# Two changes to one kernel: the last quarter of x is turned by VectorE and moved by transfers, and the first transfers wait for one another

## The chip, the cores and the metric

The kernel runs on one core of one Trainium2 chip. A core has TensorE (PE), VectorE (DVE), ScalarE (ACT), GpSimd (POOL) and SyncE (SP), each with its own instruction queue, and 16 DMA engines that all queues share. The time is device microseconds of one execution. The kernel before takes 2688.36 us, the median of 3 runs (2688.32 to 2688.46).

## The reference, cut to what matters

Everything is float32, with 256 tokens of 2048 features. Two layers (a mixer and an MLP each) are followed by one hybrid layer of attention and gating. What matters here is that each of the five stages begins by normalizing x and multiplying it by a large weight matrix:

```python
def rms_norm(x, g):
    xf = x.astype(jnp.float32)
    y = xf * lax.rsqrt(jnp.mean(xf * xf, axis=-1, keepdims=True) + EPS)
    return (y * g.astype(jnp.float32)).astype(x.dtype)

def sq_relu_mlp(h, w1, w2):
    a = jax.nn.relu(jnp.einsum("btd,df->btf", h, w1))
    return jnp.einsum("btf,fd->btd", a * a, w2)

def first_block(x, ...):
    for layer in range(DEPTH):                       # DEPTH = 2
        h = rms_norm(x, mix_pre_g[layer])
        if layer % 2 == 0:
            m = pool_conformer_mixer(h, ...)         # window means, a causal convolution of 31 taps, layer norm, silu
        else:
            m = short_conv_mixer(h, ...)             # gates and a causal convolution of 3 taps
        x = x + rms_norm(m, mix_post_g[layer])
        h = rms_norm(x, ffn_pre_g[layer])
        x = x + rms_norm(sq_relu_mlp(h, ffn_w1[layer], ffn_w2[layer]), ffn_post_g[layer])
    return x

def hybrid_layer(x, norm_g, w_in, ...):
    proj = rms_norm_2(x, norm_g) @ w_in              # 2048 x 11264
    ...                                              # attention of 8 heads, spatial gating
    return x + merged @ w_out
```

## The kernel before

**Stages, chunks and steps.** The work on TensorE is 160 chunks of 512 output columns, in five stages: stage 0 is the first mixer, 1 its MLP, 2 the second mixer, 3 its MLP, 4 the hybrid layer. A chunk contracts 1024 or 2048 rows of a weight matrix in steps of 256 rows (`STEP_K = 2` blocks of 128). `SEQ` is the list of all steps (chunk, i), `POS` the place of a step in it, and a stage's first step is called f here. In stages 1 to 4 the first two chunks are interleaved: f to f+3 are steps 0 to 3 of the first, f+4 to f+7 steps 0 to 3 of the second, f+8 to f+11 steps 4 to 7 of the first, f+12 to f+15 those of the second.

**The exact product.** Each float32 operand is held as a rounded part (hi) and the rest (lo), and a product is three matmuls (L786 to L788): `w_hi` by `A_lo`, `w_lo` by `A_hi`, `w_hi` by `A_hi`. For each of the 2 token tiles and 2 blocks that makes 12 matmuls of 512 columns in a step. ScalarE makes `w_hi` (`split_hi`, L747), VectorE `w_lo` (`split_lo`, L765), in 6 slots; both run 3 steps ahead of the step that they stand at (`split_steps`, `AHEAD`). Some steps are split in two halves (L735, L755), those in `HALVED` among them. SyncE loads two steps at a time (1 MB) into 3 slots (`load_weights`, L627), each load behind a wait on `lo_made` for the slot's last use. `load_rows` (L637) loads 128 rows (256 KB) with a semaphore of its own.

**The left operand.** x lies token by token in SBUF; `A_hi` and `A_lo` need it feature by feature and scaled by the gain. Its 2048 features are 4 groups of 512 (g = 0 to 3). TensorE transposes a group in 16 blocks of 128x128 for stages 1 to 4, groups 0 and 1 tile by tile in `boundary` (L854), groups 2 and 3 by `turn_x` (8 each, L837) between steps: group 2 behind step f+4, group 3 behind step f+6. ScalarE reads the bank and writes `A_hi` (`hi_x`, L1083 and L1084), VectorE writes `A_lo` (`lo_x`, L1468). Group 2 is first used in step f+8, group 3 in step f+10. At step f+8 ScalarE also runs `statistics` (L1125), the sums of squares of the two tiles.

**What sets the order.** It is written out by hand: every engine's program walks the same list of steps and does its extra work at named (chunk, i). Engines meet on semaphores alone. In hidden layers VectorE also transposes 32x32 blocks itself (`turn_blocks`, L1839): one instruction takes 32 partitions and puts the result on another 32, 16 of them for a group.

**The opening.** SyncE issues the first transfers one behind the other with no wait: the rows of steps 0 to 3 by `load_rows`, quarters of x by `load_x` (L614), one load of 1 MB in two pieces, then 14 small transfers of parameters (L659 to L673), and only then the load of steps 6 and 7, which waits for `lo_made` too. ScalarE's queue issues one transfer, the first eighth of x (L1162). TensorE transposes the parameters (13 transfers) behind step 5 of chunk 0.

**The convolution's end.** In chunks 6 to 9 of stage 0 VectorE's last taps (`DVE_TAP_TO` = 58), the layer norm at (8, 2) and the silu at (9, 1) and (10, 0) have their places; TensorE transposes the convolution's result for the norm behind (8, 2), at L940.

Of the kernel before, what the change touches and what calls it, by code (L numbers as in the profile page):

```python
# [251 lines left out]
def build(nc, t):  # L252
    ctx = ExitStack()
    with ctx:
# [62 lines left out]
        for name in ("A", "B"):  # L317
            halves[name] = tuple(sbuf(f"{name}_{h}", D // P * TOK, F32R).rearrange("p (k t) -> p k t", t=TOK)
                                 for h in ("hi", "lo"))
# [52 lines left out]
        x_begun = semaphore("x_begun")  # L372


        BEGIN = 2 * STEPS_PER_LOAD
        rows_loaded = [semaphore(f"rows_loaded{i}") for i in range(2 * GK)]
# [235 lines left out]
        def sync_program(e):  # L612
# [47 lines left out]
            e.dma_start(rows[32:64, 0:P], t["ffn_pre_g"].rearrange("l (k p) -> (l k) p", p=P)).then_inc(par_loaded, 16)  # L660
            for name, key in (("norm_g_2", "pre2"), ("pool_scale", "pool_scale"), ("conv_b", "conv_b"),
                              ("conv_ln_g", "ln_g"), ("conv_ln_b", "ln_b"), ("q_norm_g_2", "q_g"), ("k_norm_g_2", "k_g")):
                n = t[name].shape[1] // P
# [1511 lines left out]
```

## Time and profile before

| what | value |
|---|---|
| median of 3 runs | 2688.36 us (2688.32 to 2688.46) |
| the profiled execution's own time | 2690.7 us |
| its span, first to last instruction | 2689.0 us |
| granted TensorE clock | 1.000 of full speed |
| TensorE busy | 2679.8 us, 12001 matmuls (weight loads 2218.5 us beside them) |
| VectorE busy | 1872.4 us (70%) |
| ScalarE busy | 1292.8 us (48%) |
| GpSimd busy | 278.2 us (10%) |
| DMA | 515.58 MB, mean 192 GB/s; SyncE's queue fills 55.4% of the 16 engines' span |

TensorE is busy in every one of the page's 40 slices at 90% or more. The difference between the profiled execution and the median is 2.3 us, and the span leaves 1.7 us of the execution outside. A matmul's end is modelled, so a row's duration overlaps the next row's start; the pace is read from start to start.

### The profile page before, as it was taken

What the parts mean: (1) busy time and instruction counts of PE and PEld (TensorE: products, weight loads), DVE (VectorE), ACT (ScalarE), POOL (GpSimd) and SP (SyncE); (2) the same over time, 40 slices, a digit from 0 to 9 for tenths busy, and PEclk for the clock granted to TensorE, in tenths of its full rate; (3) what the DMA queues carried; (4) which work ended last, traced back from release to release, by engine and by line L of the source; (5) the groups of instructions that cost most, each with busy time, mean ns of one, the idle gap of its engine ahead of it and who ended that gap; (6) DMA issues with size and microseconds to landing.
All of it is one profiled execution on the core that took longest, in us unless ns stands there. A gap on an engine that the chain in (4) does not pass through costs nothing.

```text
span 2689.0 us, 31099 instructions
## 1 busy us (share of the span) xinstructions
PE 2679.8 (100%) x12001; PEld 2218.5 (83%) x12001; DVE 1872.4 (70%) x2495; ACT 1292.8 (48%) x1635; POOL 278.2 (10%) x263
## 2 busy tenths in 40 slices
PE   9999999999999999999999999999999999999999
PEld 7888888888888888888888888888888888888887
DVE  6878777666866767776677676667767757765564
ACT  6765544434444454444544444344445446544452
POOL 4851100000000010000110000000011001000000
PEclk9999999999999999999999999999999999999999
DMA  7545665555555556555555555555555645455554
GB/s 248 183 169 180 215 211 183 184 202 188 193 192 195 194 183 213 193 197 194 187 188 204 203 188 186 190 188 203 188 188 179 211 173 182 169 200 194 188 188 156
DMA packets 267972, 515.58 MB, mean 192 GB/s; under 512 B 8450, under 2 KB 27956, under 8 KB 267316
## 3 DMA queue, kind: packets, MB, share of 16 engines
q1 hardware_dynamic: 267556, 513.34, 55.4%
q8 instruction: 98, 1.61, 0.2%
q14 instruction: 46, 0.38, 0.0%
q10 hardware_dynamic: 272, 0.26, 0.0%
HBM read 511.47 MB, written 2.10 MB: 191 GB/s over the span
## 4 chain that ended last, share of the span: by engine, by line
PE 98%; DMA 1%; DVE 1%; ACT 0%; issue 0%; SPq 0%
PE bank L786 32%; PE bank L788 32%; PE bank L787 32%; PE bank L837 1%; DMA x_res<-in_x 0%; DMA w_raw<-in_ab_w_in 0%; PE bank L854 0%; PE bank L1027 0%; DVE w_lo L765 0%; PE bank L988 0%; PE bank L1041 0%; PE bank L1014 0%; DVE w_lo L755 0%; DVE bank L1783 0%; PE bank L1048 0%
## 5 line engine op out<-in xcount | busy, mean ns | idle before, releaser
L765 DVE TENSOR_TENSOR w_lo<-w_raw,w_hi 128x1024 fp32r<-128x1024 f32 x952 | 1183.1, 1265 | 493.5 <-ACT w_hi L747 487.8
L747 ACT ACTIVATE w_hi<-w_raw 128x1024 fp32r<-128x1024 f32 x956 | 974.7, 1056 | 589.9 <-PE bank L788 432.9
L786 PE MATMUL bank<-w_hi,A_lo 128*128 128x512 f32 x2432 | 952.5, 392 | 2.3 <-DVE A_lo L1468 0.8
L788 PE MATMUL bank<-w_hi,A_hi 128*128 128x512 f32 x2432 | 947.2, 389 | 0.0
L787 PE MATMUL bank<-w_lo,A_hi 128*128 128x512 f32 x2432 | 946.7, 389 | 0.0
L786 PE MATMUL bank<-w_hi,B_lo 128*128 128x512 f32 x1408 | 548.7, 390 | 0.0
L788 PE MATMUL bank<-w_hi,B_hi 128*128 128x512 f32 x1408 | 547.9, 389 | 0.0
L787 PE MATMUL bank<-w_lo,B_hi 128*128 128x512 f32 x1408 | 547.8, 389 | 0.0
L786 PEld LDWEIGHTS bank<-w_hi,A_lo 128*128 128x128 f32 x2432 | 456.6, 188 | 98.4 <-DVE w_lo L765 2.3
L788 PEld LDWEIGHTS bank<-w_hi,A_hi 128*128 128x128 f32 x2432 | 456.4, 188 | 95.8
L787 PEld LDWEIGHTS bank<-w_lo,A_hi 128*128 128x128 f32 x2432 | 456.7, 188 | 93.2
L788 PEld LDWEIGHTS bank<-w_hi,B_hi 128*128 128x128 f32 x1408 | 264.3, 188 | 54.9
L786 PEld LDWEIGHTS bank<-w_hi,B_lo 128*128 128x128 f32 x1408 | 264.3, 188 | 54.7
L787 PEld LDWEIGHTS bank<-w_lo,B_hi 128*128 128x128 f32 x1408 | 264.3, 188 | 54.6
L1072 ACT ACTIVATE z<-bank,small 128x512 f32<-128x512 f32 x108 | 68.4, 685 | 341.9 <-PE bank L788 341.8
L1839 DVE STREAM_TRANSPOSE conv_out<-z 32x256 f32<-32x256 f32 x512 | 222.9, 435 | 10.5
L2131 POOL TENSOR_TENSOR z<-z 128x512 f32<-128x512 f32 x64 | 65.2, 1040 | 1105.5 <-ACT z L1072 1105.5
L1866 DVE TENSOR_TENSOR acc<-bank,acc 128x512 f32<-128x512 f32 x96 | 61.9, 686 | 85.7 <-PE bank L788 85.7
L2012 POOL TENSOR_TENSOR acc<-acc,gain_row 128x512 f32<-128x512 f32 x32 | 40.9, 1294 | 518.7 <-ACT bank L1131 483.5
L1425 ACT ACTIVATE B_hi<-conv_out 128x512 fp32r<-128x512 f32 x64 | 37.0, 628 | 100.2 <-DVE conv_out L1839 100.2
L1131 ACT ACTIVATE bank<-acc 128x512 f32<-128x512 f32 x32 | 19.0, 595 | 79.9 <-DVE acc L1521 51.1
L2006 POOL TENSOR_TENSOR small<-small,neg_half 128x1 f32<-128x1 f32 (+2 forms) x21 | 23.3, 1110 | 307.8 <-DVE small L1460 288.9
(178 smaller groups left out, 975.7 us busy)
## 6 DMA issues: line engine op xcount, KB each, us to landing
w_raw<-in_ffn_w SPq DMA_DIRECT2D x256, 1024.0 KB, 5.1
w_raw<-in_w_in SPq DMA_DIRECT2D x88, 1024.0 KB, 4.9
w_raw<-in_sc_w_in SPq DMA_DIRECT2D x48, 1024.0 KB, 5.1
w_raw<-in_ab_w_out SPq DMA_DIRECT2D x16, 1024.0 KB, 5.0
w_raw<-in_sc_w_out SPq DMA_DIRECT2D x16, 1024.0 KB, 5.1
w_raw<-in_w_out SPq DMA_DIRECT2D x16, 1024.0 KB, 5.3
w_raw<-in_ab_w_in SPq DMA_DIRECT2D x28, 512.0 KB, 4.6
w_raw<-in_ab_w_in SPq DMA_DIRECT2D x8, 1024.0 KB, 5.1
```

The source lines that it names most:

```text
L747: e.activation(w_hi[:, s % SPLIT_SLOTS, :], raw_step(s), ACT.Copy).then_inc(hi_made, 1)
L765: e.tensor_tensor(w_lo[:, slot, :], raw_step(s), w_hi[:, slot, :].bitcast(F32), ALU.subtract).then_inc(lo_made, 1)
L786: e.matmul(ps, lo[:, kt, tok], wh, start=first, stop=False)
L787: e.matmul(ps, hi[:, kt, tok], wl, start=False, stop=False)
L788: ins = e.matmul(ps, hi[:, kt, tok], wh, start=False, stop=last)
L837: ins = e.transpose(view[:, k, tt * P:(tt + 1) * P], src(tt, slice(f, f + P)), ident)
L1072: e.activation(out(tt), main_bank(c, tt), func, scale=rs(layer_of(c))[:, tt:tt + 1]).then_inc(act_took(c, tt), 1)
L1425: e.activation(halves["B"][0][:, kt:kt + 2, :], h_T[:, 2 * h:2 * h + 2, :], ACT.Copy).then_inc(hi_cast("h", layer, b, j, h), 1)
L1839: ins = e.transpose(dst[feat, :, :].rearrange("p k (t c) -> p t k c", t=NT)[:, :, :, tok], src[tok, :, :].rearrange("p t (k c) -> p t k c" ...
L1866: e.tensor_tensor(out, main_bank(c, tt), out, ALU.add).then_inc(dve_took(c, tt), 1)
L2012: e.tensor_tensor(out, out, gain_row[:, c], ALU.mult).then_inc(gained(p, n, tt), 1)
L2131: e.tensor_tensor(z[:, s, tt, :], z[:, s, tt, :], z[:, s, tt, :], ALU.mult).then_inc(squared(layer, b, j, tt), 1)
```

## The change

**For stages 1 to 4, group 3 of x.** At the end of VectorE's `boundary` the new `turn_last` transposes it with 4 instructions on 128 partitions, each 32x32 block within its own band of 32 partitions, into `x_quads` (a part of `conv_in`). The new `move_x` then sends the 16 blocks of 32 partitions by 256 elements (32 KB each) to the bands where they belong, into `x_T` (a part of `conv_out`), from ScalarE's queue: 6 behind step f+4, 6 behind f+5, 4 behind f+6 in ScalarE's program. At step f+8 ScalarE waits for all 16 and makes `A_hi` (`hi_moved`, 4 activations from SBUF), VectorE makes `A_lo` (`lo_moved`, 8 instructions of 128x128), both ahead of the statistics. `turn_x(p, 3)` and the `hi_x`, `lo_x` of group 3 are gone, and two banks less are filled in a stage.

**In the opening**, most of SyncE's first transfers wait for an earlier one to have landed, the third load is made of `load_rows` too (so steps 4 and 5 are split in halves), and the parameters come behind the loads of steps 6 to 9. ScalarE and VectorE take the splits of steps 2 and 3 between the two halves of group 1. The parameters' transposes stand one step later.

**In stage 0's end**, VectorE does the last two steps' taps together one step earlier, its norm one step earlier, and the first silu is one step earlier on three engines.

```diff
     for key in turn_order():
+        if key[0] == "pre" and key[1] > 0 and key[2:3] == (NG - 1,):
+            continue
...
+        x_quads = conv_in_flat[:, 0:GK * TOK]
+        x_T = conv_out_flat[:, GK * TOK:2 * GK * TOK]
...
-        BEGIN = 2 * STEPS_PER_LOAD
+        BEGIN = RAW_SLOTS * STEPS_PER_LOAD
...
             load_rows(0, 0)
             load_rows(0, 1)
             e.dma_start(x[:, :, CH // 2:CH], x_dram[:, :, CH // 2:CH]).then_inc(x_loaded[0], 16)
+            e.wait_ge(x_begun, 16)
             load_rows(0, 2)
+            e.wait_ge(rows_loaded[0], 16)
             load_rows(0, 3)
+            e.wait_ge(rows_loaded[1], 16)
             load_x(1)
-            for k in range(GK):
-                load_rows(1, k)
+            e.wait_ge(x_loaded[0], 16)
+            load_rows(1, 0)
+            e.wait_ge(rows_loaded[2], 16)
+            load_rows(1, 1)
+            e.wait_ge(rows_loaded[3], 16)
+            load_rows(1, 2)
+            load_rows(1, 3)
+            e.wait_ge(x_loaded[1], 16)
             load_x(2)
-            load_weights(2)
+            e.wait_ge(rows_loaded[4], 16)
+            load_rows(2, 0)
...
+            e.wait_ge(x_loaded[2], 16)
             load_x(3)
-            e.dma_start(rows[0:32, 0:P], t["mix_pre_g"]...
...
             for n in range(RAW_SLOTS, LOADS):
                 load_weights(n)
+                if n == RAW_SLOTS + 1:
+                    load_params()
...
-                if (c, i) == (0, 5):
+                if (c, i) == (0, 6):
                     e.wait_ge(par_loaded, 16 * 13)
...
-                if c == up_chunk(layer, 0, 1) and i in (0, 2):
-                    turn_x(p, 2 + i // 2)
+                if (c, i) == (up_chunk(layer, 0, 1), 0):
+                    turn_x(p, 2)
...
+            def move_x(p, blocks):
+                e.wait_ge(x_turned.sem, x_turned.of(p))
+                for q, r in (divmod(m, 4) for m in blocks):
+                    e.dma_start(x_T[32 * r:32 * r + 32, q * TOK:(q + 1) * TOK],
+                                x_quads[32 * q:32 * q + 32, r * TOK:(r + 1) * TOK]).then_inc(x_moved, 16)
+            def hi_moved(p):
+                e.wait_ge(x_moved, 256 * p)
+                for k in range(GK):
+                    kt = GK * (NG - 1) + k
+                    ins = e.activation(by_32(halves["A"][0][:, kt, :]), moved(k), ACT.Copy, scale=par_col(PRE_COL[p], kt))
...
-                if (c, i) == (STAGE[p] + 1, 2):
-                    hi_x(p, 3)
+                if (c, i) in MOVE_AT[p]:
+                    move_x(p, MOVE_AT[p][c, i])
                 if (c, i) == (STAGE[p], 4):
+                    hi_moved(p)
                     statistics(p)
...
+        MOVE_AT = {p: {(STAGE[p] + 1, i): range(6 * i, min(6 * i + 6, 16)) for i in range(3)} for p in range(1, 5)}
...
+            def turn_last(p):
+                e.wait_ge(x_made.sem, x_made.of(p - 1, NG - 1, 1))
+                blocks = x[:, :, (NG - 1) * CH:].rearrange("p t (k c) -> p t k c", k=GK)
+                for r in range(4):
+                    out = x_quads[:, r * TOK:(r + 1) * TOK].rearrange("p (t k c) -> p t k c", t=NT, k=GK)
+                    ins = e.transpose(out, blocks[:, :, :, 32 * r:32 * r + 32])
+                ins.then_inc(x_turned(p), 1)
...
-                if (c, i) == (8, 2):
+                if (c, i) == (8, 1):
                     dve_norm(e, mean)
-                if (c, i) in ((9, 1), (10, 0)):
+                if (c, i) in ((9, 0), (10, 0)):
                     dve_silu(e, c - 9)
```

How the order of instructions moves is shown at three places. The first is ScalarE at the start of stage 1, from the end of group 2's `A_hi` to the statistics, before:

```order
210 L1084 ACTIVATE A_hi<-bank,par 128x256
211 L747 ACTIVATE w_hi<-w_raw 128x1024 x2
212 L1083 ACTIVATE A_hi<-bank,par 128x256
213 L1084 ACTIVATE A_hi<-bank,par 128x256
214 L1083 ACTIVATE A_hi<-bank,par 128x256
215 L1084 ACTIVATE A_hi<-bank,par 128x256
216 L747 ACTIVATE w_hi<-w_raw 128x1024 x2
217 L1125 ACTIVATE acc,small<-x_res 128x2048 x2
218 L747 ACTIVATE w_hi<-w_raw 128x1024 x3
```

And the same place in the changed kernel, where `conv_out` is `x_T` and `conv_in` is `x_quads`:

```order
211 L1111 ACTIVATE A_hi<-bank,par 128x256
212 L1125 DMA conv_out<-conv_in 32x256 x6
213 L774 ACTIVATE w_hi<-w_raw 128x1024
214 L1125 DMA conv_out<-conv_in 32x256 x6
215 L774 ACTIVATE w_hi<-w_raw 128x1024
216 L1125 DMA conv_out<-conv_in 32x256 x4
217 L774 ACTIVATE w_hi<-w_raw 128x1024 x2
218 L1133 ACTIVATE A_hi<-conv_out,par 128x256 x4
219 L1171 ACTIVATE acc,small<-x_res 128x2048 x2
220 L774 ACTIVATE w_hi<-w_raw 128x1024 x3
```

The 16 issues stand between the splits of weights, and the four activations of group 3 have moved behind four splits, directly ahead of the statistics. The second place is VectorE at the end of stage 1's boundary, before:

```order
175 L1543 SCALAR_TENSOR_TENSOR x_res<-acc,small,x_res 128x512 x2
176 L765 TENSOR_TENSOR w_lo<-w_raw,w_hi 128x1024
177 L1543 SCALAR_TENSOR_TENSOR x_res<-acc,small,x_res 128x512 x2
178 L765 TENSOR_TENSOR w_lo<-w_raw,w_hi 128x1024 x2
179 L1468 SCALAR_TENSOR_TENSOR A_lo<-bank,par,A_hi 128x256 x4
180 L765 TENSOR_TENSOR w_lo<-w_raw,w_hi 128x1024 x2
181 L1468 SCALAR_TENSOR_TENSOR A_lo<-bank,par,A_hi 128x256 x4
182 L765 TENSOR_TENSOR w_lo<-w_raw,w_hi 128x1024 x2
183 L1460 TENSOR_SCALAR small<-small 128x2
```

And the same place in the changed kernel:

```order
178 L1627 SCALAR_TENSOR_TENSOR x_res<-acc,small,x_res 128x512 x2
179 L1545 STREAM_TRANSPOSE conv_in<-x_res 128x256 x4
180 L792 TENSOR_TENSOR w_lo<-w_raw,w_hi 128x1024 x2
181 L1527 SCALAR_TENSOR_TENSOR A_lo<-bank,par,A_hi 128x256 x4
182 L792 TENSOR_TENSOR w_lo<-w_raw,w_hi 128x1024 x4
183 L1555 SCALAR_TENSOR_TENSOR A_lo<-conv_out,par,A_hi 128x128 x8
184 L1519 TENSOR_SCALAR small<-small 128x2
```

Four transposes stand ahead of the splits of steps f+6 and f+7, and group 3's `A_lo` is 8 smaller instructions behind step f+11's split. The third place is SyncE's opening, before:

```order
5 L614 DMA x_res<-in_x 128x2x512
6 L637 DMA w_raw<-in_ab_w_in 128x2x256 x4
7 L614 DMA x_res<-in_x 128x2x512
8 L627 DMA w_raw<-in_ab_w_in 128x4x256 x2
9 L614 DMA x_res<-in_x 128x2x512
10 L659 DMA z<-in_mix_pre_g 32x128
```

And in the changed kernel, with the semaphore that each issue waits for:

```order
4 L643 DMA w_raw<-in_ab_w_in 128x2x256 [waits x_begun]
5 L643 DMA w_raw<-in_ab_w_in 128x2x256 [waits rows_loaded0]
6 L620 DMA x_res<-in_x 128x2x512 [waits rows_loaded1]
7 L643 DMA w_raw<-in_ab_w_in 128x2x256 [waits x_loaded0]
8 L643 DMA w_raw<-in_ab_w_in 128x2x256 [waits rows_loaded2]
9 L643 DMA w_raw<-in_ab_w_in 128x2x256 [waits rows_loaded3]
10 L643 DMA w_raw<-in_ab_w_in 128x2x256
11 L620 DMA x_res<-in_x 128x2x512 [waits x_loaded1]
```

The order of the transfers of weights and x is the same; what is new are the waits, which leave some four transfers under way at a time.

## Rows read from the trace of the kernel before

**Rows 1.** The page's part 4: the chain that ended last.

```profile
PE 98%; DMA 1%; DVE 1%; ACT 0%; issue 0%; SPq 0%
```

**Rows 2.** TensorE's opening in the timeline: start us, us, instruction [idle before it].

```profile
7.12 0.50 PE L786 MATMUL bank<-w_hi,A_lo 128*128 128x512 f32 x1 [0.66 <-DVE w_lo L755]
...
10.50 0.40 PE L788 MATMUL bank<-w_hi,A_hi 128*128 128x512 f32 x1
12.63 1.09 PE L837 MATMUL bank<-ident,x_res 128*128 128x128 f32 x8 [1.73 <-DMA x_res<-in_x]
...
23.93 0.50 PE L786 MATMUL bank<-w_hi,A_lo 128*128 128x512 f32 x1 [0.67 <-DVE w_lo L765]
...
31.93 0.47 PE L786 MATMUL bank<-w_hi,A_lo 128*128 128x512 f32 x1 [0.81 <-DVE A_lo L1468]
...
34.77 0.39 PE L786 MATMUL bank<-w_hi,A_lo 128*128 128x512 f32 x1
```

**Rows 3.** DMA busy share in one stretch of the opening (windows view).

```profile
core 0: us, PE busy (x) PEld busy (x) DVE busy (x) ACT busy (x) POOL busy (x), PEclk, DMA share, GB/s
10.00:12.50 2.50, 0.90 (x4) 0.38 (x3) 1.72 (x4) 1.51 (x3) 2.21 (x12) 1.00 1.07 371
```

**Rows 4.** Transfers by line: size of one, median us from issue to landing.

```profile
w_raw<-in_ffn_w SPq DMA_DIRECT2D x256, 1024.0 KB, 5.1
...
out_x<-x_res SPq DMA_DIRECT2D x8, 256.0 KB, 2.1
x_res<-in_x SPq DMA_DIRECT2D x3, 512.0 KB, 8.8
...
x_res<-in_x ACTq DMA_DIRECT2D x1, 256.0 KB, 3.6
...
sgu_row<-in_sgu_norm_g SPq DMA_DIRECT2D x1, 64.0 KB, 6.2
```

**Rows 5.** SyncE's issues in the opening (timeline).

```profile
13.41 0.56 SPq L659 DMA_DIRECT2D z<-in_mix_pre_g  x1
14.02 0.42 SPq L660 DMA_DIRECT2D z<-in_ffn_pre_g  x1
14.48 0.43 SPq L664 DMA_DIRECT2D z<-in_norm_g  x1
...
18.84 37.86 SPq L627 DMA_DIRECT2D w_raw<-in_ab_w_in  x18
```

**Rows 6.** TensorE at the start of stage 1 (timeline).

```profile
267.60 1.03 PE L837 MATMUL bank<-ident,x_res 128*128 128x128 f32 x8
268.39 0.47 PE L786 MATMUL bank<-w_hi,A_lo 128*128 128x512 f32 x1
...
283.01 0.39 PE L786 MATMUL bank<-w_hi,A_lo 128*128 128x512 f32 x1
...
288.45 0.39 PE L786 MATMUL bank<-w_hi,A_lo 128*128 128x512 f32 x1
```

**Rows 7.** ScalarE: its one transfer, then the start of stage 1 (timeline).

```profile
0.80 0.44 ACTq L1162 DMA_DIRECT2D x_res<-in_x  x1
...
269.68 2.02 ACT L747 ACTIVATE w_hi<-w_raw 128x1024 fp32r<-128x1024 f32 x2
...
277.94 1.93 ACT L1125 ACTIVATE acc<-x_res 128x2048 f32<-128x2048 f32 x1
```

**Rows 8.** VectorE at the start of stage 1 (timeline).

```profile
267.24 2.36 DVE L765 TENSOR_TENSOR w_lo<-w_raw,w_hi 128x1024 fp32r<-128x1024 f32 x2
...
282.82 3.50 DVE L765 TENSOR_TENSOR w_lo<-w_raw,w_hi 128x1024 fp32r<-128x1024 f32 x3 [0.78 <-ACT w_hi L747]
```

**Rows 9.** Costliest groups, by line: count, busy us, mean ns of one.

```profile
L1839 DVE STREAM_TRANSPOSE conv_out<-z 32x256 f32<-32x256 f32 x512 | 222.9, 435 | 10.5
```

**Rows 10.** One line's instructions: ns min/median/max, first and last start.

```profile
L1483 DVE SCALAR_TENSOR_TENSOR A_lo<-bank,par,A_hi x64: 340/344/351, 251.3 to 2016.2; 128x128 fp32r<-128x128 f32 x64
```

**Rows 11.** Waits of TensorE: us in total, times, longest.

```profile
PE bank L940 <- DVE conv_out L1769: 0.3, 1, 0.3
```

More of the change, by code:

```diff
@@ L371, in build @@
         x_loaded = [semaphore(f"x_loaded{i}") for i in range(NG)]
[L372 to L376 removed]
+        x_begun, x_moved = semaphore("x_begun"), semaphore("x_moved")
+        BEGIN = RAW_SLOTS * STEPS_PER_LOAD
+        rows_loaded = [semaphore(f"rows_loaded{i}") for i in range(RAW_SLOTS * GK)]
         half_hi = semaphore("half_hi")
@@ L448, in build @@
                                    ([(g, tt) for tt in tiles for g in gs] if 0 in gs else [(g, tt) for g in gs for tt in tiles])])
+        x_turned = signal("x_turned", [(p,) for p in range(1, 5)])
         tap_done = signal("tap_done", DVE_TAPS)
@@ L660, in sync_program @@
[L660 to L663, printed above, removed]
-                e.dma_start(rows[ROWS[key]:ROWS[key] + n, 0:P],
-                            t[name].rearrange("l (k p) -> (l k) p", p=P)).then_inc(par_loaded, 16)
@@ L666, in sync_program @@
-            e.dma_start(rows[ROWS["b_spatial"]:ROWS["b_spatial"] + 8, 0:P], t["b_spatial_2"][0, :, :]).then_inc(par_loaded, 16)
-            taps = t["conv_w"].rearrange("l k (b p) -> (l k b) p", p=P)
-            for h in two:
-                e.dma_start(rows[0:CONV_ROWS, (1 + h) * P:(2 + h) * P],
-                            taps[h * CONV_ROWS:(h + 1) * CONV_ROWS, :]).then_inc(par_loaded, 16)
-            e.dma_start(rows[0:SHORT_ROWS, 3 * P:4 * P],
-                        t["sc_conv_w"].rearrange("l k (b p) -> (l k b) p", p=P)).then_inc(par_loaded, 16)
@@ L966, in pe_program @@
                 r = c - C_L2
-                if r == 1 and i in (0, 2):
-                    turn_x(4, 2 + i // 2)
+                if (r, i) == (1, 0):
+                    turn_x(4, 2)
                 if since(c, i, C_L2) == 3:
@@ L1170, in act_program @@
                 at[0] += 1
-            hi_x(0, 1)
+            for h in two:
+                hi_half(0, 1, h)
+                split_to(e, split_hi, at, STEPS_PER_LOAD + h)
             for c, i in split_steps(e, 0, split_hi, at):
@@ L1186, in act_program @@
                     hi_x(0, 2 + i // 4)
-                if (c, i) == (0, 5):
+                if (c, i) == (0, 6):
+                    statistics(0)
                     e.wait_ge(aux_filled.sem, aux_filled.of("rows"))
@@ L1470, in lo_scaled, with lo_half, lo_moved @@
                 ins.then_inc(lo_cast(*key), 1)
+            def lo_half(p, g, h):
+                kt = GK * g + 2 * h
+                lo_scaled("A", kt, [par_col(PRE_COL[p], kt + k) for k in two], "pre", p, g, h)
             def lo_x(p, g):
                 for h in two:
-                    kt = GK * g + 2 * h
-                    lo_scaled("A", kt, [par_col(PRE_COL[p], kt + k) for k in two], "pre", p, g, h)
+                    lo_half(p, g, h)
+            def turn_last(p):
[5 more added lines that the diff above has]
+                ins.then_inc(x_turned(p), 1)
+            def lo_moved(p):
+                hi, lo = halves["A"]
+                for k in range(GK):
+                    kt = GK * (NG - 1) + k
+                    e.wait_ge(hi_cast.sem, hi_cast.of("pre", p, NG - 1, k // 2))
+                    for tt in tiles:
+                        ins = e.scalar_tensor_tensor(by_32(lo[:, kt, :])[:, tt, :, :], moved(k)[:, tt, :, :],
+                                                     par_col(PRE_COL[p], kt), by_32(hi[:, kt, :].bitcast(F32))[:, tt, :, :],
+                                                     ALU.mult, ALU.subtract)
+                    if k % 2 == 1:
+                        ins.then_inc(lo_cast("pre", p, NG - 1, k // 2), 1)
             def lo_part(p, g, tt, h):
@@ L1589, in dve_program @@
                 at[0] += 1
-            lo_x(0, 1)
+            for h in two:
+                lo_half(0, 1, h)
+                split_to(e, split_lo, at, STEPS_PER_LOAD + h)
             for c, i in split_steps(e, 0, split_lo, at):
```

64 lines of the change are left out of this document (46 added, 18 removed).

## The prediction

> **What bounds the kernel now.** I read the chain that ended last first: 98% of the span is TensorE [rows 1]. So a change is worth only what it takes out of TensorE's stream, or what it stops TensorE from waiting for. The second view is TensorE's timeline, read from start to start. In stage 1, 24 matmuls lie between the starts 283.01 and 288.45 us [rows 6], 0.227 us each, so a step of 12 takes 2.72 us; there the stream has no holes. The third is the same view of the opening [rows 2]: between the first product at 7.12 and the start of the eighth step at 34.77 there are three waits, 1.73 us for x (group 1), 0.67 for `w_lo` and 0.81 for `A_lo`. The brackets count from a modelled end: the start at 10.50 and one pace of 0.23 give 10.73, and the next start is 12.63, so the hole is 1.90, 0.17 more than its bracket. With 0.17 added to each, the three are 1.9 + 0.84 + 0.98 = 3.7 us. One wait of 0.3 us stands at the end of stage 0, ahead of the norm's transposes [rows 11]. The fourth view is what the other engines do at a stage's start [rows 7, 8], since the change loads both.
>
> **The opening.** Before, the transfers are issued without waits and share the engines: the DMA share is 1.07 at 371 GB/s [rows 3], and a quarter of x (512 KB) takes 8.8 us to land, against 5.1 for 1 MB later [rows 4]. Group 1 lands late since later transfers move beside it. With the waits it is issued when the second 256 KB of weights has landed. From ScalarE's row, 256 KB land 3.6 us after issue [rows 4]; for the second row load, issued at about 1.8, I estimate 5.5, so group 1 goes out at about 5.9. Ahead of it and beside it are at most 1.25 MB issued from 4.4 on (0.80 + 3.6, the first landing). At 371 GB/s these take 3.4 us, and the fixed part of a landing is 2.1 less 0.7 of moving [rows 4], 1.4: it lands at 4.9 + 3.4 + 1.4 = 9.7. TensorE asks for it at about 10.5. So the first hole goes.
> The third hole goes too. The load of steps 6 and 7 is issued at 18.84 [rows 5], behind parameters whose issue began at 13.41; SyncE spent 5.4 us on 14 of them. Now it is issued when group 3 has been, by my estimate near 16, and TensorE needs it near 28. What is late next is step 4: VectorE splits it behind group 2's `A_lo`, in halves, so I leave 0.3 us of the second hole. The parameters, 5.4 us of issues, begin near 18 and end near 23.5; with the 6.2 us of the one in the crowd [rows 4] they land by 30, and TensorE asks near 31. Queued behind them on SyncE is the load of steps 10 and 11, which TensorE needs near 39. Sum: -3.7 + 0.3 = -3.4 us. Bounds: the opening's 27.65 us hold seven steps of 2.72, 28 transposes of 0.1 (below) and four small ones, 22.3 in all, so no more than 5.3 can go; and if x still takes 8.8 us from its issue at 5.9, it lands at 14.7, 2.1 later than now, which the third hole's 1 us partly pays: +1.1. I take 3.4, since the page shows what crowded the transfer.
>
> **The end of stage 0.** Earlier taps end the 0.3 us wait [rows 11]: -0.3. VectorE then stands in its norm one step earlier while the split of one step waits behind it; that split costs it 1.2 us, and I see no reason for a new wait above 0.3. Bounds -0.3 and +0.3.
>
> **What goes at stages 1 to 4.** Eight transposes behind step f+6. Group 2's eight start at 267.60, the next product at 268.39 [rows 6]: 0.79 us for eight. Four stages: -3.2 us. The two banks fewer, the later waits on `lo_cast` and GpSimd's wait for the moves stand where nothing is near, and cost nothing.
>
> **What comes to VectorE.** Four transposes on 128 partitions. The row for 32 partitions and the same 256 elements has 435 ns [rows 9]; all partitions work at once, so 4 x 0.435 = 1.75 us. Bounds: nothing less than half of that, and 0.75 each (3 us) if one costs what 128x512 costs it. They stand ahead of the splits of f+6 and f+7, which begin at 267.24 [rows 8]. So f+6's `w_lo`, 1.2 us, ends near 270.3 instead of 268.4; TensorE needs it at 268.39 + 2.75 = 271.1. That is covered by 0.8 us; at 3 us of transposes it would be 0.5 late. `A_lo` of group 3 becomes 8 instructions of 128x128, 0.344 each [rows 10], 2.3 to 2.8 us in all, of which four stand between the landing and step f+10.
>
> **What comes to ScalarE.** This is the term that decides. Sixteen issues: its one transfer has 0.44 us, the two of 32 and 16 rows on SyncE have 0.42 and 0.43 and start 0.46 apart [rows 5, 7], so 0.47 each and 7.5 us a stage. Group 2's `A_hi` ends and the issues can begin at 269.7 [rows 7]. Queued behind them are `w_hi` of f+8 to f+11 (0.98 each, 3.9 in all), group 3's `A_hi` (four, 1.5 us), the statistics (3.8, from 277.94 to 281.7) and then `w_hi` of f+12. Two ends:
> Overlapped: an issue occupies the queue, not the datapath, so the activations already handed over run under the next issues. The last issue ends at 269.7 + 7.5 = 277.2, lands 2.1 us later [rows 4] at 279.3, and `A_hi` of group 3 ends at 280.8. For step f+10 the first half needs 0.85 for `A_hi` and 1.3 for `A_lo`: ready at 281.5. TensorE wants it at 283.01 - 0.79 = 282.2 [rows 6]. The statistics start at 280.8 instead of 277.94, 2.9 late. `w_lo` of f+12 was ready at 284.0 [rows 8] for a start at 287.7, a cover of 3.6: no wait.
> In a row: 269.7 + 7.5 + 3.9 = 281.1 for f+11's `w_hi`, the last issue at 279.2, landed 281.3. Step f+10 is ready at 283.4, 1.2 late; the statistics start at 282.8, 4.9 late, and f+12 waits 1.3 in all (the two are not added). A stage then nets -0.8 + 1.3 = +0.5.
> The rows show no transfer issued beside activations on ScalarE, so this is bounded, not read. I take the first end, since issues are not part of ScalarE's busy time, and since activations here start 0.36 us apart though one lasts 0.47: the engine does take its next work early. The stages give -3.2.
> The Trainium skill ("Perfetto Trace Analysis", Per-instruction lifecycle) says that a ScalarE instruction is pushed into a wait queue and leaves the sequencer free, while a transfer is held by the sequencer until its descriptors are made. By that rule the first end holds, by a plain in-order reading the second; no run here shows it. Against the change speaks another page, "DMA: Bandwidth & Descriptors", Bandwidth: transfers under 64 KB are dominated by descriptors, and 1 MB or more should be batched. Here each move has 32 KB; the nearest row, 256 KB in 2.1 us, would make that a matter of the last landing alone, so the rule would change the third rival's chance and not the sum.
>
> **The sum.** -3.4 - 0.3 - 3.2 = -6.9 us. The profiled execution took 2690.7, which becomes 2683.8; it is 2.3 above the median of the runs, so the forecast is 2688.4 - 6.9 = 2681.5 us.
>
> **Rivals.**
> 1. Issues and activations in a row (above): -3.4 - 0.3 + 4 x 0.5 = -1.7, 2686.7 us. For it: queues are in order, and 7.5 us of issues is more than ScalarE's idle time in the three steps. Against it: the busy count leaves issues out.
> 2. The opening gives little, the stages all: the waits leave the DMA engines idle between transfers and group 1 lands near 12, so 1.0 us remains of the gain. -1.0 - 0.3 - 3.2 = -4.5, 2683.9 us. For it: each wait adds a landing and an issue. Against it: some 1 MB stays under way.
> 3. Slower: the last moves land late. Weights of 1 MB are loaded beside them, and a transfer of 64 KB in a crowd took 6.2 us [rows 4]. In a row, the last issue at 279.2 lands at 285.4, step f+10 is ready at 287.5 instead of 282.2: 5.3 us, less 0.8, four times +4.5 = +18, with -3.7 elsewhere +14.3: 2702.7 us. A stage's wait at f+10 is the landing less 0.85 in a row, less 2.85 overlapped; the change stops gaining from a wait of 1.7 (a landing of 2.6 or 4.6 us) and costs 0.2% from one of 3.1 (3.9 or 5.9 us). Against it: ScalarE's queue is its own, and 256 KB on it landed in 3.6 us while SyncE's were under way.
> That the turned blocks aren't there in time because VectorE is late is the 0.5 us above; it would give 2683.5 and stays inside the range.
>
> **How the numbers follow.** A measurement of this kernel can tell 0.2%, 5.4 us, from no change: under 2683.0 is faster, over 2693.8 slower. Forecast 0.50, rival 1 0.27, rival 2 0.13, rival 3 0.10. Faster: the forecast's case but for its edge, where the opening gives under 1.9 (0.46), and 0.07 of rival 2, whose time lies 0.9 above the line: 0.53. Slower: 0.09 of rival 3, which also holds milder cases. Same: the rest, 0.38. The range reaches down to the opening's bound of 5.3 (2679.6) and up past rival 1 with a stage net of +1 (2688.7): 2679.6 to 2688.7. The likeliest case alone has 2679.6 to 2683.6.
>
> **What would show it.** Right: TensorE's waits in the first 35 us sum to under 0.5, and the eighth step starts near 31.4 instead of 34.77; no wait of TensorE near f+10 or f+12 in any of four stages; ScalarE's `w_hi` rows overlap the issues in time; the issues last about 0.44; the transposes on 128 partitions about 0.44; group 3's `A_hi` starts at f+8 plus 1.5 to 2.5 us. Wrong: a row in which TensorE waits for `A_lo` or `w_lo` four times by over 1 us (rival 1 at 1.3, rival 3 at 5), for x in the opening (rival 2), or for the parameters' transfers.

## The result, and the profile after

The changed kernel takes 2699.1 us (median of 6 runs, 2698.3 to 2701.8) where the kernel before took 2688.3 beside it (6 runs, 2687.6 to 2688.7). The ratio is 1.0043, with a 95% interval from 1.0032 to 1.0054: slower by 10.8 us. The forecast was 2681.5, with 2679.6 to 2688.7 as its range. The profiled execution of after took 2700.25 us, with a span of 2698.5; before's had 2690.7 and 2689.0, so the two differ by 9.5.

The page's chain that ended last, which answers to [rows 1], is the first sign: TensorE has 96% of it instead of 98%, and ScalarE's transfers and ScalarE itself have come in with 1% each.

```profile
PE 96%; ACTq 1%; DMA 1%; DVE 1%; ACT 1%; issue 0%; SPq 0%; POOL 0%
```

TensorE's waits in the whole program (us in total, times, longest) say where:

```profile
PE bank L813 <- DVE A_lo L1555: 9.4, 4, 4.3
PE bank L813 <- DVE A_lo L1527: 1.6, 1, 1.6
...
PE bank L864 <- DMA x_res<-in_x: 1.5, 1, 1.5
...
PE bank L813 <- DVE w_lo L792: 0.5, 1, 0.5
```

L1555 is the `A_lo` of the turned group 3, and TensorE waits for it four times, once in each of stages 1 to 4: the row that the prediction named as the sign that its forecast is wrong. The wait of [rows 11] for `conv_out` is gone, but a new one of 0.5 us for `w_lo` (L792) has come at 206.40. (L813 to L815 are the three matmuls that were L786 to L788, and L1527 is the `A_lo` that was L1468.)

To see which stretch loses, I take the start of the first eight transposes of each stage (before and after, from the timelines) and the span's end.

| stretch | before, start | after, start | change in length |
|---|---|---|---|
| opening and stage 0 | 0 | 0 | -0.7 |
| stage 1 | 250.27 | 249.60 | +0.8 |
| stage 2 | 950.77 | 950.94 | +5.2 |
| stage 3 | 1304.03 | 1309.43 | +1.1 |
| stage 4, to the end | 2004.46 | 2010.98 | +3.0 |

In stage 1, TensorE's timeline (start us, us, instruction, idle before it) answers to [rows 6]:

```profile
266.88 1.03 PE L864 MATMUL bank<-ident,x_res 128*128 128x128 f32 x8
...
283.08 0.47 PE L813 MATMUL bank<-w_hi,A_lo 128*128 128x512 f32 x1 [1.52 <-DVE A_lo L1555]
```

The eight transposes of group 3 are gone (0.79 us), and a hole of 1.52 + 0.17 = 1.7 us has come at step f+10: together +0.9, where the table has +0.8. ScalarE beside it, which answers to [rows 7]:

```profile
268.10 0.59 ACTq L1125 DMA_DIRECT2D conv_out<-conv_in  x1
...
268.73 3.17 ACTq L1125 DMA_DIRECT2D conv_out<-conv_in  x5
272.01 1.06 ACT L774 ACTIVATE w_hi<-w_raw 128x1024 fp32r<-128x1024 f32 x1 [2.92 <-issue]
272.03 3.73 ACTq L1125 DMA_DIRECT2D conv_out<-conv_in  x6
275.81 1.06 ACT L774 ACTIVATE w_hi<-w_raw 128x1024 fp32r<-128x1024 f32 x1 [2.74 <-issue]
275.83 2.49 ACTq L1125 DMA_DIRECT2D conv_out<-conv_in  x4
278.43 2.01 ACT L774 ACTIVATE w_hi<-w_raw 128x1024 fp32r<-128x1024 f32 x2 [1.56 <-issue]
280.35 1.70 ACT L1133 ACTIVATE A_hi<-conv_out,par 128x256 fp32r<-128x256 f32 x4
```

Two things are to be read here. The activation at 272.01 and the issues at 272.03 run side by side: an activation handed over doesn't hold the issues behind it. But the next activation stands behind all six of those issues, and starts at 275.81, when they are out, after 2.74 us of idling for "issue". And the 16 issues take 0.59 + 3.17 + 3.73 + 2.49 = 9.98 us, 0.62 each. The row of the moves over the whole program (ns min/median/max), and the one from issue to landing:

```profile
L1125 ACTq DMA_DIRECT2D conv_out<-conv_in x64: 514/612/1403, 268.1 to 2039.7; - x64
...
DMA to landing us min/median/max: 1.9/3.4/5.9
```

VectorE at the same place answers to [rows 8] and [rows 9]:

```profile
266.64 1.42 DVE L1545 STREAM_TRANSPOSE conv_in<-x_res 128x256 f32<-128x256 f32 x4
...
279.52 2.36 DVE L792 TENSOR_TENSOR w_lo<-w_raw,w_hi 128x1024 fp32r<-128x1024 f32 x2 [1.39 <-ACT w_hi L774]
281.80 2.18 DVE L1555 SCALAR_TENSOR_TENSOR A_lo<-conv_out,par,A_hi 128x128 fp32r<-128x128 f32 x8
```

In stage 2 ScalarE's last issues end at 980.4, its two `w_hi` at 982.5, and then it waits for a landing:

```profile
977.07 3.33 ACTq L1125 DMA_DIRECT2D conv_out<-conv_in  x4
980.50 2.01 ACT L774 ACTIVATE w_hi<-w_raw 128x1024 fp32r<-128x1024 f32 x2 [2.40 <-PE bank L815]
984.98 1.70 ACT L1133 ACTIVATE A_hi<-conv_out,par 128x256 fp32r<-128x256 f32 x4 [2.47 <-DMA conv_out<-conv_in]
```

TensorE's hole is 4.5 us there, and what follows it runs slow; the last row is the hole of stage 4:

```profile
987.20 0.63 PE L813 MATMUL bank<-w_hi,A_lo 128*128 128x512 f32 x1 [4.31 <-DVE A_lo L1555]
987.62 0.63 PE L814 MATMUL bank<-w_lo,A_hi 128*128 128x512 f32 x1
...
990.61 0.48 PE L815 MATMUL bank<-w_hi,A_hi 128*128 128x512 f32 x1
990.92 0.40 PE L813 MATMUL bank<-w_hi,A_lo 128*128 128x512 f32 x1
...
2045.05 0.47 PE L813 MATMUL bank<-w_hi,A_lo 128*128 128x512 f32 x1 [1.88 <-DVE A_lo L1555]
```

The windows view (the last three columns are granted clock, DMA share, GB/s) shows the lower level of TensorE's clock, 0.50 or 1.2 GHz, behind the holes of stages 2 and 4:

```profile
986.00:988.00 2.00, 0.80 (x2) 0.70 (x3) 2.00 (x8) 2.00 (x3) 0.00 (x0) 0.84 1.04 401
988.00:990.00 2.00, 2.00 (x6) 1.58 (x5) 0.10 (x1) 2.00 (x3) 0.00 (x0) 0.50 0.15 57
...
2046.00:2048.00 2.00, 2.00 (x6) 1.54 (x6) 0.17 (x1) 2.00 (x3) 0.00 (x0) 0.50 1.03 398
```

Between 987.20 and 990.61 eight products start 0.427 us apart instead of 0.227: 1.6 us, and about as much again in stage 4. Behind the holes of stages 1 and 3 (1.52 and 1.71 in the timeline) the clock stays at 1.00. So a stage's change is -0.8 for the transposes, plus the hole, plus the slow stretch: -0.8 + 4.5 + 1.7 = +5.4 in stage 2, -0.8 + 2.05 + 1.7 = +3.0 in stage 4. The table has +5.2 and +3.0, so the account closes within 0.2 us.

The opening answers to [rows 2 to 5]. TensorE's holes, three of SyncE's rows, and the median landing of x's quarters (8.8 us in [rows 4]):

```profile
11.79 1.09 PE L864 MATMUL bank<-ident,x_res 128*128 128x128 f32 x8 [1.50 <-DMA x_res<-in_x]
...
30.27 0.47 PE L813 MATMUL bank<-w_hi,A_lo 128*128 128x512 f32 x1 [1.62 <-DVE A_lo L1527]
```

```profile
5.76 0.37 SPq L620 DMA_DIRECT2D x_res<-in_x  x1
...
17.94 2.37 SPq L633 DMA_DIRECT2D w_raw<-in_ab_w_in  x4
20.36 2.67 SPq L646 DMA_DIRECT2D z<-in_mix_pre_g  x1
```

```profile
x_res<-in_x SPq DMA_DIRECT2D x3, 512.0 KB, 5.7
```

Group 1 of x is issued at 5.76, close to the 5.9 of the forecast, but TensorE gets it at 11.79, 6.0 us later, against 12.63 in [rows 2]. The load of steps 6 and 7 is issued at 17.94, only 0.9 us ahead of [rows 5]. ScalarE splits it from 25.88 (it had waited 3.41 us for it), so the third hole isn't gone: it is 1.6 us. The eighth step starts at 33.72, where the forecast wanted 31.4 and [rows 2] have 34.77. The third hole differs from execution to execution: over the six traces with all the new waits it runs from none (the loads held) to 2.7 us (the filled holes).

### The profile page after: what moved, and what is told of

Same layout as the page of the kernel before. It is cut to its first block, busy times and chain, and to the rows that moved or that the text cites. A ratio compares the mean times of both kernels' runs of the same rounds, so it can differ in the third digit from the quotient of the medians.

```text
span 2698.5 us, 31133 instructions
## 1 busy us (share of the span) xinstructions
PE 2679.9 (99%) x11969; PEld 2216.8 (82%) x11969; DVE 1881.9 (70%) x2529; ACT 1294.7 (48%) x1637; POOL 281.7 (10%) x263
## 4 chain that ended last, share of the span: by engine, by line
PE 96%; ACTq 1%; DMA 1%; DVE 1%; ACT 1%; issue 0%; SPq 0%; POOL 0%
PE bank L813 31%; PE bank L815 31%; PE bank L814 31%; ACTq L1125 1%; ACT w_hi L774 0%; DVE w_lo L792 0%; DMA x_res<-in_x 0%; DMA w_raw<-in_ab_w_in 0%; PE bank L881 0%; PE bank L864 0%; PE bank L1054 0%; DMA conv_out<-conv_in 0%; DVE A_lo L1555 0%; PE bank L1015 0%; PE bank L1068 0%
## 5 line engine op out<-in xcount | busy, mean ns | idle before, releaser
L792 DVE TENSOR_TENSOR w_lo<-w_raw,w_hi 128x1024 fp32r<-128x1024 f32 x950 | 1182.2, 1265 | 502.0 <-ACT w_hi L774 496.3
L813 PE MATMUL bank<-w_hi,A_lo 128*128 128x512 f32 x2432 | 953.9, 392 | 11.8 <-DVE A_lo L1555 9.4
L815 PE MATMUL bank<-w_hi,A_hi 128*128 128x512 f32 x2432 | 948.4, 390 | 0.0
L813 PE MATMUL bank<-w_hi,B_lo 128*128 128x512 f32 x1408 | 548.8, 390 | 0.5 <-DVE w_lo L792 0.5
L815 PE MATMUL bank<-w_hi,B_hi 128*128 128x512 f32 x1408 | 547.8, 389 | 0.0
L813 PEld LDWEIGHTS bank<-w_hi,A_lo 128*128 128x128 f32 x2432 | 457.4, 188 | 110.1 <-issue 12.0
L815 PEld LDWEIGHTS bank<-w_hi,A_hi 128*128 128x128 f32 x2432 | 457.2, 188 | 95.9
L813 PEld LDWEIGHTS bank<-w_hi,B_lo 128*128 128x128 f32 x1408 | 264.3, 188 | 55.5 <-DVE w_lo L792 1.0
L815 PEld LDWEIGHTS bank<-w_hi,B_hi 128*128 128x128 f32 x1408 | 264.3, 188 | 55.0
```

Source lines behind the costliest of these rows:

```text
L792: e.tensor_tensor(w_lo[:, slot, :], raw_step(s), w_hi[:, slot, :].bitcast(F32), ALU.subtract).then_inc(lo_made, 1)
L813: e.matmul(ps, lo[:, kt, tok], wh, start=first, stop=False)
L815: ins = e.matmul(ps, hi[:, kt, tok], wh, start=False, stop=last)
```

## The experiments

Each is compared with runs of the kernel before taken beside it: 2688.32 us for the first four experiments (median of 21), 2688.24 for the next four (28), 2688.33 for the last three (15). Ratios are to these. What was expected stands ahead of each result.

**The stages alone, and the opening alone.** The first is the kernel before with the changed stages, the second the kernel before with the new opening and end of stage 0; the core of each edit:

```diff
-                if c == up_chunk(layer, 0, 1) and i in (0, 2):
-                    turn_x(p, 2 + i // 2)
+                if (c, i) == (up_chunk(layer, 0, 1), 0):
+                    turn_x(p, 2)
...
+                if (c, i) in MOVE_AT[p]:
+                    move_x(p, MOVE_AT[p][c, i])
...
+                    hi_moved(p)
...
+                turn_last(p)
...
+                    lo_moved(p)
```

```diff
             load_x(1)
+            e.wait_ge(x_loaded[0], 16)
+            load_rows(1, 0)
+            e.wait_ge(rows_loaded[2], 16)
+            load_rows(1, 1)
...
+                if n == RAW_SLOTS + 1:
+                    load_params()
...
-                if (c, i) == (8, 2):
+                if (c, i) == (8, 1):
```

> Only the part for stages 1 to 4 is changed, the opening and stage 0 are as before. Theory 1 (the loss is all in the four stages: 16 issues of 0.61 us each on ScalarE's queue and landings of 3 to 5 us make group 3's A_lo late for step f+10): 10 to 12 us slower than before, holes of TensorE of 1.5 to 4.5 us ahead of step f+10, four times. Theory 2 (the loss needs the changed opening or stage 0 too, by a shift against the load of weights): under 6 us slower, holes under 1 us.

> Only the opening and the end of stage 0 are changed, stages 1 to 4 are as before. Theory 1: 0.7 us faster than before (2687.7), as the first block of stage 1's transposes started 0.67 us earlier in the changed kernel's trace; the waits in the opening only change their places. Theory 2 (the forecast's): 3.4 to 3.7 us faster (2684.8). Theory 3 (the opening's other shape sets off the later loss): slower than before by several us.

The stages alone: 2698.55 us, ratio 1.0039 (1.0025 to 1.0052). The opening alone: 2689.27, ratio 1.0005 (0.9996 to 1.0014). So the whole loss lies in stages 1 to 4, as theory 1 of the first had it. The opening has no gain that can be measured: both the 0.7 us and the 3.4 us of its first two theories failed. TensorE's waits in each, the stages first:

```profile
PE bank L792 <- DVE A_lo L1533: 8.0, 4, 2.9
```

```profile
PE bank L807 <- DVE A_lo L1509: 1.6, 1, 1.6
PE bank L858 <- DMA x_res<-in_x: 0.9, 1, 0.9
PE bank L807 <- DVE w_lo L786: 0.5, 1, 0.5
```

**All moves from SyncE's queue.** This takes the issues out of ScalarE's stream and leaves all else:

```diff
                 load_weights(n)
+                for p in range(1, 5):
+                    if n == S0[STAGE[p]] // STEPS_PER_LOAD + 5:
+                        e.wait_ge(x_turned.sem, x_turned.of(p))
+                        for q, r in (divmod(m, 4) for m in range(16)):
+                            e.dma_start(x_T[...], x_quads[...]).then_inc(x_moved, 16)
...
-                if (c, i) in MOVE_AT[p]:
-                    move_x(p, MOVE_AT[p][c, i])
```

> The changed kernel, with the 16 moves issued from SyncE's queue in one go, behind the load of steps f+10 and f+11, instead of from ScalarE's. Theory 1 (ScalarE's queue is what is late: w_hi and group 3's activations stand behind the issues): the issues on SyncE end near 0.45 to 0.6 x 16 behind the turn, 275.5 to 278 in stage 1, the landing by 280.5, hole of TensorE gone or under 0.5 us, 9 to 12 us faster than the changed kernel (2687 to 2690). Theory 2 (the issue of a move from SBUF to SBUF costs 0.6 us on any queue and lands after 3 to 6 us beside the loads): the last landing is no earlier, the holes stay over 1 us in at least two stages, under 5 us faster.

2691.97 us, ratio 1.0015 (1.0005 to 1.0024): 7 us faster than the changed kernel, still slower than before. SyncE's row in stage 1, how long the moves take to land, and TensorE's waits:

```profile
268.46 10.09 SPq L705 DMA_DIRECT2D conv_out<-conv_in  x16
...
279.23 2.07 SPq L633 DMA_DIRECT2D w_raw<-in_ffn_w  x3
```

```profile
DMA to landing us min/median/max: 1.8/1.8/3.1
```

```profile
PE bank L819 <- DVE w_lo L798: 3.5, 3, 1.7
PE bank L819 <- DVE A_lo L1559: 2.5, 3, 1.4
```

An issue of such a move takes 0.63 us on this queue too: the price belongs to the move and not to ScalarE. The load of weights behind them goes out at 279.23 instead of 270.34, and TensorE waits for `w_lo` of that load in stages 1 and 3, 1.7 and 1.3 us (the row's third wait is the 0.5 of stage 0's end). It still waits for group 3's `A_lo` too, 0.2, 0.9 and 1.4 us in stages 1, 2 and 4. The chain has only changed its queue. The gain of 7 us lies between the two theories: the price of an issue is theory 2's, but the landing was not late here.

**Filled holes.** TensorE runs idle transposes where the holes are, which leaves the waits and takes away the slow stretch:

```diff
+        FILL = (0, 14, 40, 14, 16)
...
+                if (c, i) == (STAGE[p], 5):
+                    for _ in range(FILL[p]):
+                        e.transpose(aux_bank("pre", p, 2, 1)[:, 0:P], ident, ident)
```

> The changed kernel; TensorE runs 14, 40, 14 and 16 transposes of the identity into a free bank behind step f+9 of stages 1 to 4, about as long as the holes there were. Theory 1 (a hole of 1.9 us or more lets the granted clock fall to half for some 3.5 us after it, in stages 2 and 4): no stretch at half clock, the waits for A_lo shorter by the filling, the time 3 to 4 us less than the changed kernel's, 2695 to 2696. Theory 2 (the clock's fall has nothing to do with the hole): half clock as before, the time the same or up to 1 us more.

2697.84 us, ratio 1.0037 (1.0023 to 1.0051), 1.3 under the changed kernel, where 3 to 4 were expected; the two intervals overlap. In its trace the 40 transposes stand where the hole was and the product behind them takes 0.47 us, not 0.63:

```profile
983.87 4.53 PE L987 MATMUL bank<-ident 128*128 128x128 f32 x40
988.25 0.47 PE L813 MATMUL bank<-w_hi,A_lo 128*128 128x512 f32 x1
```

Stage 2 takes 357.0 us instead of 358.5 and stage 4 685.4 instead of 687.5: 3.7 us for the two. Stage 3 is 0.6 longer and the opening of this execution 1.0 longer, so the spans differ by 2.0 us. The clock's share in the loss is shown in the two traces; the medians can't confirm its size.

**The moves split over two queues**, eight on SyncE's (at the place of the experiment above) and eight on ScalarE's, with the new opening and with the old one:

```diff
+                        for q, r in (divmod(m, 4) for m in range(8)):
...
-        MOVE_AT = {p: {(STAGE[p] + 1, i): range(6 * i, min(6 * i + 6, 16)) for i in range(3)} for p in range(1, 5)}
+        MOVE_AT = {p: {(STAGE[p] + 1, i): range(8 + 4 * i, 12 + 4 * i) for i in two} for p in range(1, 5)}
```

> Changed kernel, but eight of the 16 moves of a stage go out from SyncE's queue (behind the load of steps f+10 and f+11) and eight from ScalarE's (four in each of two steps). Theory 1, the loss is the chain of issues, 0.63 us each on either queue, with one landing behind it: eight issues are 5.0 us a queue, the last ScalarE issue ends near 275, group 3's A_hi begins by 278 even with a landing of 3.5 us, SyncE's next load is 3 us late instead of 9 and nobody waits for it. All holes at f+10 and f+12 go and the clock stays at 1.00: 2699.1 - 10.1 (four holes) - 3.6 (two stretches at the lower clock) = 2685.4 us, 2.9 under before. Theory 2, the loss is the work on the turned blocks itself (128x128 pieces of A_lo and the statistics behind them): waits of 1 us or more for A_lo or w_lo stay in each stage, 2690 to 2693.

> As the split of the moves over two queues, but with the opening and the end of stage 0 of the kernel before. Theory 1, the new opening gives nothing that lasts (its gain of 0.9 us in one trace is within what the opening varies by): within 1 us of the split with the new opening. Theory 2, the new opening does give its 3.4 us and was hidden by something else: 2 to 4 us slower than the split with the new opening.

2686.24 us with the new opening, ratio 0.9993 (0.9984 to 1.0002), and 2684.68 with the old one, ratio 0.9986 (0.9978 to 0.9995). The second is the version that beats both kernels, by 3.6 us and 14 us. In neither trace does TensorE wait at f+10 or f+12. ScalarE in stage 1 of the second:

```profile
268.81 1.06 ACT L759 ACTIVATE w_hi<-w_raw 128x1024 fp32r<-128x1024 f32 x1 [1.91 <-PE bank L800]
268.83 2.46 ACTq L1110 DMA_DIRECT2D conv_out<-conv_in  x4
271.34 2.96 ACT L759 ACTIVATE w_hi<-w_raw 128x1024 fp32r<-128x1024 f32 x3 [1.47 <-PE bank L800]
274.20 1.70 ACT L1118 ACTIVATE A_hi<-conv_out,par 128x256 fp32r<-128x256 f32 x4
```

Group 3's `A_hi` starts 9.5 us behind the transposes of group 2 (264.69), where the changed kernel had 280.35 - 266.88 = 13.5; TensorE wants step f+10 at 14.5. That leaves room even for one move of this execution that landed after 5.2 us: ScalarE waited 1.6 us for it, TensorE didn't. Stages 1 to 4 are 0.91, 0.96, 0.84 and 0.60 us shorter than in the trace of before, 3.3 in all. The old opening is 1.6 us better than the new one here, which neither theory had; the two intervals overlap.

**The loads held.** SyncE sends its next load of weights only when the moves have landed:

```diff
                 load_weights(n)
+                for p in range(1, 5):
+                    if n == S0[STAGE[p]] // STEPS_PER_LOAD + 5:
+                        e.wait_ge(x_moved, 256 * p)
```

> Changed kernel, all 16 moves on ScalarE's queue, but SyncE holds its next 1 MB load until the moves of the stage have landed. Theory 1, the moves land late because 1 MB loads move beside them: from issue to landing median 1.8 to 2.2 us and at most 3, as on SyncE's queue where no load was issued between them; the A_lo wait of stage 2 falls from 4.3 to under 2.5; w_lo waits of 2 to 5 us appear at the step of the load held, so the whole is slower, 2700 to 2715. Theory 2, the landing is late because of ScalarE's queue itself: median 3.4 and up to 5.9 as before, and the wait of stage 2 stays at 4.

2700.05 us (median of 3), ratio 1.0040 (1.0025 to 1.0055). The profiled execution took 2696.91, the lowest of the three. Landings and waits:

```profile
DMA to landing us min/median/max: 1.8/1.9/3.0
```

```profile
PE bank L816 <- DVE A_lo L1558: 7.2, 4, 2.2
PE bank L816 <- DVE w_lo L795: 1.9, 3, 0.8
```

The landing falls from 3.4 to 1.9 us on the same queue, so it was the 1 MB loads beside the moves that made it late, as theory 1 had it; the waits for `w_lo` are smaller than its 2 to 5 us. Stage 2's wait falls from 4.3 to 2.2, and `A_hi` no longer waits for a transfer there; stages 1, 3 and 4 keep 1.5, 1.6 and 1.9 us. The late landing was 2.1 us of stage 2; the rest of all four holes stands with no landing waited for, behind the chain of issues.

**One wait in the opening**, in the kernel before with the new opening: of the waits between transfers only those up to group 1 stay.

```diff
             load_x(1)
-            e.wait_ge(x_loaded[0], 16)
             load_rows(1, 0)
-            e.wait_ge(rows_loaded[2], 16)
...
-            e.wait_ge(x_loaded[2], 16)
             load_x(3)
```

> Before with the changed opening and end of stage 0, but of the opening's waits between transfers only those ahead of x's group 1 stay; the second load's rows, group 2, the third load's rows and group 3 are issued at once. Theory 1, the waits leave the DMA engines idle (255, 290, 276 GB/s between 5 and 20 us where 311, 369, 232 stood): group 1 still lands near 12, the loads behind it 1 to 3 us earlier, the hole ahead of step 6 (1.6 us at 30) goes to under 0.5, TensorE's waits of the opening sum to 2.0 or less. Theory 2, what crowds a transfer is what is issued behind it: group 1 lands after 13, its hole is 2.5 us or more, and the opening ends no earlier. The whole time moves by under 2 us either way, 2687 to 2691.

2688.00 us, ratio 0.9999 (0.9990 to 1.0008). From 10 to 20 us the DMA engines move 352 and 359 GB/s, where the opening alone had 301 and 302, and the hole at 30 us is gone; group 1 comes at 12.04, 0.4 later, with 1.6 us of waiting. The waits do leave the DMA engines idle, but without them the opening is only as good as the old one.

```profile
10.00:15.00 5.00, 3.38 (x19) 2.63 (x18) 3.11 (x7) 2.99 (x8) 4.36 (x33) 1.00 1.03 352
15.00:20.00 5.00, 5.00 (x27) 4.21 (x26) 3.02 (x7) 2.32 (x6) 3.27 (x7) 1.00 1.09 359
```

**Before, profiled again, twice**, and at last the split with the opening of one wait:

> The kernel before, unchanged, for a second profile of its opening. Two kernels whose opening is word for word that of before began stage 1's transposes at 247.75 and 247.38 us, the profile of before at 250.27. Theory 1, the opening differs from execution to execution: this one begins stage 1 earlier than 249.5, with holes that sum to less than 3 us before the eighth step, so that the 3.7 us of holes which the forecast wanted to win were partly those of one execution. Theory 2, the opening repeats itself: 250.3 within 0.3, the same three holes.

> The kernel before once more, a third profile. The same two theories: earlier than 249.5 by the first, 250.3 within 0.3 by the second.

> The split of the moves over two queues, with the new opening of which only the wait ahead of x's group 1 is kept. Theory 1, the stages alone make the difference and no form of the opening is worth anything measurable: 2684 to 2686 us, within 1 us of the split with the old opening (2684.7). Theory 2, the waits between the later transfers cost 1 to 2 us of what the opening has to give: 2683 or less, under both other splits.

The two executions of before took 2687.94 and 2688.69 us, and stage 1's first transposes start at 247.66 and 248.40, where the first profile had 250.27. TensorE's holes in the opening of the second profile, from the first product on, which answer to [rows 2]:

```profile
11.04 1.09 PE L837 MATMUL bank<-ident,x_res 128*128 128x128 f32 x8 [0.42 <-DMA x_res<-in_x]
22.25 0.50 PE L786 MATMUL bank<-w_hi,A_lo 128*128 128x512 f32 x1 [0.67 <-DVE w_lo L765]
```

The wait for x of 1.73 us was that of one execution; here it is 0.42, and in the third profile there is none. The split with one wait took 2684.79 us, ratio 0.9987 (0.9978 to 0.9996), the same as with the old opening. Over five traces with before's opening (the two with the stages' change among them) stage 1 starts at 247.4 to 250.3, 248.3 in the mean; over six with all the new waits at 248.2 to 250.6, 249.4 in the mean; over two with one wait at 247.8 and 248.0.

## Why the prediction was wrong, point by point

**What bounds the kernel: right.** TensorE's stream decides, and every microsecond of the loss is a hole or a slow stretch in it.

**The opening, -3.4: wrong, it gives nothing (+1.0 alone, within its interval of -1.1 to +3.8).** Two steps failed. The first is "it lands at 4.9 + 3.4 + 1.4 = 9.7": it landed near 11.8, since the transfers that wait for one another move 255 GB/s from 5 to 10 us, and not the 371 that the sum took. (The sum's 4.9 doesn't follow from its own 4.4 either; with 4.4 it would be 9.2, further off.) That was rival 2, with its time for this hole ("lands near 12") met. The second is the 3.7 us to be won, which came from a profiled execution that lay 2.3 above the median. The prediction said so, but took the excess off the whole and left the holes at their size. The excess was in those very holes; in two more profiles they sum to 1.4 and 2.2 us (brackets of 0.42 and 0.67; of 0.20, 0.67 and 0.78; 0.17 added to each). The lower bound was too low for the same reason.

**The end of stage 0, -0.3: the wait went, and another came,** 0.5 us for `w_lo`, above the 0.3 that was allowed for. It is in every trace with this part.

**What goes at stages 1 to 4, -3.2: right.** Where nothing waits, the four stages are shorter by 3.3 us.

**VectorE: right, and cheaper than said.** The four transposes take 1.42 us, 0.36 apart, against 1.75. `A_lo` in eight pieces took 2.18, just under its 2.3 to 2.8. TensorE waits for none of it by itself.

**ScalarE: this is the step that failed, by its size first.** "so 0.47 each and 7.5 us a stage": it was 0.62 each and 10.0 us. The choice between the ends was nearly right: an activation does run under the issues behind it. The Trainium skill ("Perfetto Trace Analysis", Per-instruction lifecycle) had this rule, and the trace agrees: 272.01 beside 272.03. What I drew from it was too much. An activation *behind* the issues isn't handed over before they are out, so the last two `w_hi`, 1.9 us, stand between the last issue (278.3) and group 3's `A_hi` (280.35) whatever has landed by then. With 0.47 an issue, the measured start gives 268.1 + 7.5 + 2.1 = 277.7 for `A_hi`, and 279.9 for step f+10, which TensorE wanted at 281.4: 1.5 us of cover. `A_hi` came 2.65 us later, and `A_lo` 0.6 more, since it stands behind two `w_lo` on VectorE until 281.80: 1.5 - 2.65 - 0.6 is the hole of 1.7. The split of the moves shows it: with eight issues a queue the holes are gone; moving all 16 elsewhere makes only another queue late; holding the loads leaves waits of 1.5 to 2.2 us in the four stages.

**The last landing, 2.1: wrong where it mattered.** The median was 3.4 us and the longest 5.9, as rival 3 feared. Its chance of 0.10 rested on "ScalarE's queue is its own", and that is no protection: the queue had nothing to do with it, the loads beside it had (1.9 us with the loads held). The Trainium skill ("DMA: Bandwidth & Descriptors", Bandwidth) says that transfers under 64 KB are dominated by their descriptors; the trace agrees in so far as the issues of these moves cost the most, 16 in a row of 0.6 us. I had made of it only a matter of the last landing.

**The result lies between rivals 1 and 3,** and neither names it: holes somewhat over rival 1's (1.2 to 1.3 forecast, 1.7, 1.9 and 2.05 measured) in stages 1, 3 and 4, and most of rival 3's (4.5 of 5.3) in stage 2. No step of the prediction had the clock: of the 9.5 us, 3.3 to 3.7 are lost by products at 1.2 GHz behind a hole. Rival 3's condition, a landing of 3.9 or 5.9 us, came close to the measured 3.4 (median) and 5.9 (longest), with a chance of only one in ten.

## What to carry to other kernels

Count the issues of a transfer cut into pieces as time in a queue, with the number of pieces times a duration measured on pieces of the same kind; what stands behind them in program order waits for all of them, whatever runs under them. Where a chain is too long for its cover, try halving it over two queues: the same 16 moves cost 10 us on ScalarE's queue and 4 on SyncE's, and gained 3.6 split over both. And a hole seen in one profiled execution is worth its full length only if the execution lies at the median: look at a second trace before counting it as a gain.

## What the runs showed of the hardware that I had not expected

- The issue of a move of 32 KB from SBUF to SBUF, on 32 partitions, has a median of 0.61 us on ScalarE's queue and 0.59 on SyncE's; ten microseconds for 16 in a row on either. The 32 and 16 rows of parameters in [rows 5] had 0.42 and 0.43.
- The same move lands in 1.8 to 1.9 us (median) when no 1 MB load goes out beside it, and in 3.4 with one, 5.9 at the longest, though the queues are different. Split over both queues, with the loads behind half of them, the median was 2.1 and the longest 5.2.
- TensorE's clock fell to 1.2 GHz behind the holes of 4.31 and 1.88 us in the changed kernel, of 2.94 and 1.84 with the stages alone and of 2.21 with the loads held; behind holes of 1.50 to 1.75, and behind one of 1.89 with the loads held, it stayed at 2.4. It also stayed there behind a hole of 2.71 in the opening (the filled holes). So the 1.9 us named ahead of that experiment is no edge, and what tells 1.88 from 1.89 stays open.
- The first transfer of the parameters took 2.67 us to issue when it stood behind a load (20.36), and 0.56 in [rows 5]. Why wasn't tried.
- Why the new opening is about 1 us worse than the old in the mean is shown only as far as the idle DMA engines go; the parts of it (the third load in rows, the parameters behind load 4) weren't tried one by one.
